# A two-layer hybrid encoder trunk on one core: tiles moved by 128 bytes, the high halves' products first, key tiles evicted in pairs

## The chip, the cores and the metric

One Trainium2 chip, one of its cores. The metric is the device time of one execution in microseconds, the median of several runs. Lower is better.

## What is computed

Two layers, each a chain of five stages on x (512 tokens, 1024 channels): a half-step SwiGLU, a mixer of three branches, a cross-attention into 256 memory tokens, a second half-step SwiGLU, and a layer norm behind each of the four residual sums.

```python
for l in range(DEPTH):                                   # DEPTH = 2
    x = layer_norm(ALPHA * x + 0.5 * swiglu(x, ffn_w12[l, 0], ffn_w3[l, 0]), ...)   # norm 0
    y = hybrid_mixer(x, ...)          # gated delta rule, RG-LRU, chunked attention, gates, w_branch, w_out
    x = layer_norm(ALPHA * x + y, ...)                                              # norm 1
    x = layer_norm(ALPHA * x + memory_cross_attention(x, mem, ...), ...)            # norm 2
    x = layer_norm(ALPHA * x + 0.5 * swiglu(x, ffn_w12[l, 1], ffn_w3[l, 1]), ...)   # norm 3
```

Everything is float32 in the reference. The kernel multiplies in a reduced float32 (fp32r): each operand is split into a high part and the rest, and a product of two is high times high, plus low times high, plus high times low, three matmuls into the same PSUM bank.

## The kernel before

**Operands.** The activations x lie as eight k tiles ("rows" below) of 128 channels by 512 tokens: `xf` whole, `xh` the high part, `xl` the rest. The weights come as a stream of 496 units of 128 x 1024 in the order of use. SP loads a unit into one of four slots of `raw`, GpSimd (`split`, L526) writes its high part to `wh` (L527) and the rest to `wl` (L529), and TensorE uses it. GpSimd may split a unit once the unit three places ahead of it has begun on TensorE (`unit_begun`, L538): then the slot's old unit is done.

**Products.** `three` (L546) issues, for one row and one output tile, `wh` with `xh`, `wh` with `xl`, `wl` with `xh`, the first name being the stationary tile and the second the moving one (the profile prints the moving tile first: `xh,wh`). `unit` (L556) does that for the rows of a unit, and a whole output tile of 128 x 512 is 24 products over eight rows. Four output tiles lie in the four banks of `acc`.

**Behind a layer norm** (`first_four`, L583) the rows of x come one by one: VectorE scales and centres a row (L1556, L1559), ScalarE applies gain and bias and writes `xh` (L1170, L1173), VectorE writes `xl` (L1552). TensorE then goes row by row over four output tiles at once, three products each. It waits for the row's `xl` before the first of them. Only in the last row does it reach the first product of tiles 1 to 3 that counts as "begun". `first_four` is called nine times: for the first feed-forward's up projection (`ffn_up0`, once at the start of the program and once behind norm 3), for `att_qk` behind norm 0, for the first four query tiles (`x_qa`) behind norm 1, for `ffn_up1` behind norm 2. A small product (`ba_product`) follows `att_qk`; in the feed-forwards the fifth tile follows at once.

**Norm 1** has company: TensorE computes the eight key tiles of the memory (`mem_k`, 256 columns, one unit each) beside it, and ScalarE evicts key tile n behind row n (`key_out`, L1408). `x_qa` begins once all eight are evicted, since it takes all four banks. It is followed by the scores and by the memory's values (`mem_v`, eight units, each used by 12 products, moving `wh`/`wl` against stationary `meh`/`mel`).

**Other users of the helpers.** The down projections (`ffn_down`, 22 rows of `hh`/`hl`), `mix_out` (`mh`/`ml`) and `x_out` (`oh`/`ol`) wait per row for the low part, before the row's first product. The mixer's branch projections read `yah`/`yal` and `ych`/`ycl`.

**Places in memory.** Tiles are laid into a partition's bytes in the order of the code, each starting at a multiple of 32. In the built program before, `xh` starts at byte 32896, `xl` at 49280, `wh` at 82048, `wl` at 98432, `const` at 114816; all of these leave 128 when divided by 256. `tmp0` starts at 120544 (leaves 224), and the other `tmp`, `y_sum` and `sq_sum` likewise. `hh` starts at 134144, `hl` at 179200, `ych` at 134144, `ycl` at 150528, `yah` at 173568, `yal` at 181760, `mh` at 189952, `ml` at 206336, `meh` at 142336, `mel` at 150528, `oh` at 183296, `ol` at 199680; all of these leave 0. Every row or column block inside a tile is a multiple of 256 bytes further on, so it leaves the same.

## Time and profile before

| | |
|---|---|
| median of 3 runs | 3358.19 us (3356.82 to 3361.05) |
| the profiled execution | 3360.91 us, its span 3359.1 us |
| TensorE busy | 94% of the span, 14648 matmuls |
| GpSimd, VectorE, ScalarE busy | 52%, 47%, 22% |
| mean granted TensorE clock | 0.974 of full |

A profile's row of a group gives its busy time, the mean of one instruction and the idle time before it. A matmul's modelled end lies behind the start of the next one, so the time per product is read from the distance of starts, or from a piece of the chain of waits divided by its count. The chain of waits is the work that ended last, followed back; in a window of it each piece has its start, its length and what it was.

### The profile page before, as it was taken

Reading aid. Unit: us, or ns where it says so; the run is one execution under the profiler, and the core shown is the slowest. Engines: PE = TensorE matmul, PEld = TensorE weight load, DVE = VectorE, ACT = ScalarE, POOL = GpSimd, SP = SyncE. Lnnn points to the kernel's source line nnn. Section 1 sums busy time; section 2 is a strip of 40 time slices with the busy share of each in tenths; the row PEclk is TensorE's granted clock in tenths of the full one; section 3 lists DMA queues with packets and bytes.
Section 4 is the critical chain, followed back from the end, with each engine's and each line's share of the span. In section 5 each row is a group of like instructions: output and inputs, shape, how many; then the busy total and the mean of one; then the engine's idle time right before and its main releaser. Section 6 shows DMA issues by size and latency. Waiting matters only on the chain.

```text
span 3359.1 us, 42233 instructions
## 1 busy us (share of the span) xinstructions
PE 3171.9 (94%) x14648; PEld 2553.5 (76%) x14648; DVE 1563.8 (47%) x1950; ACT 722.2 (22%) x1293; POOL 1763.4 (52%) x1003
## 2 busy tenths in 40 slices
PE   6999999889999898999999999998999998989996
PEld 5888765678887767888778887656888887778885
DVE  3332446855546435332244323658555373443323
ACT  1110113322221222110021102243222212221101
POOL 5666552433346655666656664424333567456662
PEclk9999999999999999999999999998999999999998
DMA  3223221111122222232222232211111223222231
GB/s 134 94 99 100 85 88 38 63 56 49 54 77 93 90 80 76 100 100 95 99 83 94 100 101 85 69 51 63 51 52 56 88 86 110 68 75 100 94 100 50
DMA packets 78864, 272.62 MB, mean 81 GB/s; under 512 B 8176, under 2 KB 12560, under 8 KB 78736
## 3 DMA queue, kind: packets, MB, share of 16 engines
q1 hardware_dynamic: 73504, 264.27, 23.7%
q10 hardware_dynamic: 5088, 5.96, 0.6%
q8 instruction: 84, 1.38, 0.2%
q0 software_dynamic: 144, 0.66, 0.0%
q14 instruction: 44, 0.36, 0.0%
HBM read 268.73 MB, written 2.12 MB: 81 GB/s over the span
## 4 chain that ended last, share of the span: by engine, by line
PE 82%; DVE 8%; issue 6%; POOL 2%; ACT 1%; DMA 0%; DVEq 0%; POOLq 0%; ACTq 0%; SPq 0%
PE acc L544 72%; PE aux L544 9%; POOL wl L529 1%; DVE dc L1634 1%; POOL wh L527 1%; DVE xl L1501 1%; DVE tmp L1689 1%; DVE dc L1632 1%; PE aux L707 1%; DVE xf L1556 0%; DMA raw<-in_stream 0%; ACT tmp L1135 0%; DVE lc L1695 0%; DVE li L1694 0%; DVE tmp L1872 0%
## 5 line engine op out<-in xcount | busy, mean ns | idle before, releaser
L527 POOL TENSOR_SCALAR wh<-raw 128x1024 fp32r<-128x1024 f32 x496 | 541.7, 1092 | 1505.1 <-PE acc L544 757.2
L529 POOL TENSOR_TENSOR wl<-raw,wh 128x1024 fp32r<-128x1024 f32 x496 | 1222.5, 2465 | 41.4
L544 PE MATMUL acc<-xh,wh 128*128 128x512 f32 x2432 | 993.2, 408 | 81.8 <-POOL wl L529 37.4
L544 PE MATMUL acc<-xh,wl 128*128 128x512 f32 x2432 | 960.4, 395 | 0.0
L544 PE MATMUL acc<-xl,wh 128*128 128x512 f32 x2432 | 960.3, 395 | 0.0
L544 PEld LDWEIGHTS acc<-xh,wh 128*128 128x128 f32 x2432 | 464.6, 191 | 211.0 <-issue 65.1
L544 PEld LDWEIGHTS acc<-xh,wl 128*128 128x128 f32 x2432 | 464.2, 191 | 100.8
L544 PEld LDWEIGHTS acc<-xl,wh 128*128 128x128 f32 x2432 | 465.4, 191 | 91.2 <-issue 2.9
L544 PE MATMUL acc<-hh,wl 128*128 128x512 f32 x704 | 278.1, 395 | 0.0
L544 PE MATMUL acc<-hh,wh 128*128 128x512 f32 x704 | 278.1, 395 | 0.0
L544 PE MATMUL acc<-hl,wh 128*128 128x512 f32 x704 | 278.1, 395 | 0.0
L1501 DVE TENSOR_TENSOR hl<-tmp,hh 128x512 f32 x88 | 228.3, 2594 | 82.2 <-ACT hh L1135 82.2
L1524 DVE SCALAR_TENSOR_TENSOR xf<-acc,xf 128x512 f32<-128x512 f32 x64 | 44.3, 692 | 383.0 <-PE acc L544 382.8
L1512 DVE TENSOR_TENSOR tmp<-tmp,acc 128x512 f32<-128x512 f32 x88 | 60.5, 688 | 275.8 <-PE acc L544 274.3
L1509 DVE SCALAR_TENSOR_TENSOR tmp<-tmp,acc 128x512 f32<-128x512 f32 x88 | 60.5, 688 | 251.1 <-ACT tmp L1135 251.1
L544 PEld LDWEIGHTS aux<-tmp 128*128 128x128 f32 x1088 | 138.3, 196 | 28.2 <-DVE tmp L1872 21.5
L1135 ACT ACT_TABLE_LOAD x85 | 109.1, 1283 | 223.0 <-PE acc L544 221.5
L544 PEld LDWEIGHTS acc<-hl,wh 128*128 128x128 f32 x704 | 132.1, 188 | 32.2
L544 PEld LDWEIGHTS acc<-hh,wl 128*128 128x128 f32 x704 | 132.1, 188 | 32.1
L544 PEld LDWEIGHTS acc<-hh,wh 128*128 128x128 f32 x704 | 132.1, 188 | 32.0
L544 PE MATMUL aux<-tmp 128*128 128x128 f32 x1088 | 142.1, 281 | 14.0 <-DVE tmp L1872 13.6
L1135 ACT ACTIVATE tmp<-xf 128x512 f32<-128x512 f32 x56 | 35.4, 633 | 539.0 <-DVE xf L1524 539.0
(266 smaller groups left out, 3780.3 us busy)
## 6 DMA issues: line engine op xcount, KB each, us to landing
raw<-in_stream SPq DMA_DIRECT2D x496, 512.0 KB, 3.4
xf<-in_xT SPq DMA_DIRECT2D x1, 2048.0 KB, 10.1
bias<-rel_scratch ACTq DMA_DIRECT2D x2, 1024.0 KB, 5.4
mraw<-in_memT ACTq DMA_DIRECT2D x2, 1024.0 KB, 5.2
out_xT<-xf SPq DMA_DIRECT2D x1, 2048.0 KB, 7.1
gate_w<-in_gate_w ACTq DMA_DIRECT2D x2, 512.0 KB, 3.5
const<-in_const POOLq DMA_DIRECT2D x1, 640.0 KB, 8.1
sc<-in_ba_w ACTq DMA_DIRECT2D x2, 256.0 KB, 2.6
```

Source lines behind the costliest of these rows:

```text
L527: pool.tensor_scalar(wh[:, s, :], raw[:, s, :], 1.0, 0.0, ALU.mult, ALU.add).then_inc(hi_step, 1)
L529: pool.tensor_tensor(wl[:, s, :], raw[:, s, :], wh[:, s, :].bitcast(F32), ALU.subtract).then_inc(unit_split, 1)
L544: return pe.matmul(out, w, x, start=start, stop=stop, skip_group_check=True)
L707: last = pe.transpose(aux[:, 2 + n % 2, j * P:(j + 1) * P], sc[:, i, j * P:(j + 1) * P], ident)
L1135: return act.activation(out, in_, func, **kw)
L1501: return tt_(dst, whole, high.bitcast(F32), ALU.subtract)
L1509: stt_(tmp[1][:, :], tmp[0][:, :], 1.0, acc[:, 2 * m, :], ALU.add, ALU.mult).then_inc(freed_d.sem, 1)
L1512: tt_(tmp[2][:, :], tmp[1][:, :], acc[:, 2 * m + 1, :], ALU.mult).then_inc(freed_d.sem, 1)
L1524: stt_(xf[:, d, :], acc[:, d % 4, :], factor, xf[:, d, :], ALU.mult, ALU.add).then_inc(freed_d.sem, 1)
L1632: return ts_(dst, src, weight(3), None, ALU.mult)
L1634: return stt_(dst[:, n:], src[:, 0:SEQ - n], weight(3 - n), dst[:, n:], ALU.mult, ALU.add)
L1689: link(dve.reciprocal(tmp[0][:, :], tmp[0][:, :]))
```

## The change

Four edits.

- A filler of 160 bytes stands behind `par`, and the filler of 32 bytes before the feed-forward's tiles is gone. `tmp`, `y_sum`, `sq_sum` and the small tiles behind them move by 160 bytes (`tmp0` to 120704, leaving 128), and everything from `hh`/`ych` on by 128 bytes (`hh` to 134272, leaving 128, and so with all the others named above). `xf` to `par` stay.
- `three` issues `wh` with `xh`, `wl` with `xh`, `wh` with `xl`. Where a row may not be there yet, TensorE waits for its high part before the first product and for its low part before the third.
- `first_four` goes over rows 0 to 5 with two products per tile (8 a row), and does the four low products of row k behind the eight of row k + 1. Rows 6 and 7 are then done tile by tile, six products each, and a tile's six begin with the product that counts as begun for tiles 1 to 3.
- Behind norm 1's row 3 ScalarE evicts key tiles 3 and 4, behind row 4 tiles 5 and 6, behind row 5 tile 7, and none behind rows 6 and 7.

```diff
+KEYS_OUT = {0: (0,), 1: (1,), 2: (2,), 3: (3, 4), 4: (5, 6), 5: (7,)}
...
         par = sb("par", [P, PAR])
+        sb("par_fill", [P, 40])
...
-        sb("line_fill", [P, 8])
...
-            def three(out, w_hi, w_lo, x_hi_, x_lo_, start, stop, begins=False):
+            def three(out, w_hi, w_lo, x_hi_, x_lo_, start, stop, begins=False, low_ready=None):
                 first = mm(out, w_hi, x_hi_, start, False)
                 if begins:
                     first.then_inc(unit_begun, 1)
-                mm(out, w_hi, x_lo_, False, False)
-                return mm(out, w_lo, x_hi_, False, stop)
+                mm(out, w_lo, x_hi_, False, False)
+                if low_ready is not None:
+                    low_ready()
+                return mm(out, w_hi, x_lo_, False, stop)
...
-            def x_ready(l, norm):
-                return lambda k: pe.wait_ge(x_lo.sem, x_lo.at(l, (norm - 1) * KD + k + 1))
+            def halves_ready(l, hi, lo, at):
+
+                def ready(k):
+                    pe.wait_ge(hi.sem, hi.at(l, at + k + 1))
+                    return lambda: pe.wait_ge(lo.sem, lo.at(l, at + k + 1))
+                return ready
...
-                ready = x_ready(l, norm)
-                for k in range(KD):
-                    ready(k)
+                ready = halves_ready(l, x_hi, x_lo, (norm - 1) * KD)
+                together = KD - 2
+                def low_row(k):
+                    low_ready[k]()
+                    for n in range(4):
+                        mm(acc[:, n, :], wh[:, n, k * P:(k + 1) * P], xl[:, k, :], False, False)
+
+                low_ready = {}
+                for k in range(together):
+                    low_ready[k] = ready(k)
+                    c = slice(k * P, (k + 1) * P)
                     for n in range(4):
                         if k == 0:
                             unit_here(l, UNIT0[name] + n)
-                        c = slice(k * P, (k + 1) * P)
-                        last = three(acc[:, n, :], wh[:, n, c], wl[:, n, c], *of_x(k), k == 0, k == KD - 1,
-                                     begins=k == (KD - 1 if n else 0))
-                        if k == KD - 1:
-                            last.then_inc(acc_ready.sem, 1)
+                        first = mm(acc[:, n, :], wh[:, n, c], xh[:, k, :], k == 0, False)
+                        if k == 0 and n == 0:
+                            first.then_inc(unit_begun, 1)
+                        mm(acc[:, n, :], wl[:, n, c], xh[:, k, :], False, False)
+                    if k:
+                        low_row(k - 1)
+                low_row(together - 1)
+                for n in range(4):
+                    unit(acc[:, n, :], n, range(together, KD), together, of_x, False, True,
+                         ready if n == 0 else None, begins=n > 0).then_inc(acc_ready.sem, 1)
...
-            def key_out(l, n):
-                tile_ready(l, "mem_k", n)
-                fn(xk[:, n, :], acc[:, n % 4, 0:MEM], ACT.Copy).then_inc(freed_a.sem, 1)
+            def keys_out(l, row):
+                for n in KEYS_OUT.get(row, ()):
+                    tile_ready(l, "mem_k", n)
+                    fn(xk[:, n, :], acc[:, n % 4, 0:MEM], ACT.Copy).then_inc(freed_a.sem, 1)
```

The same pair of waits (`halves_ready`) replaces the one wait in `ffn_down` (`hh`/`hl`), `mix_out` (`mh`/`ml`) and `x_out` (`oh`/`ol`).

**On TensorE, from the last key tile to `x_qa`.** A product reads moving tile, stationary tile; what it waits for stands in brackets. Before:

```order
L544 MATMUL acc<-mel,wh 128x256
L544 MATMUL acc<-meh,wl 128x256
L575 REGISTER_ALU
L554 REGISTER_ALU [waits x_lo,freed_a]
L544 MATMUL acc<-xh,wh 128x512 [waits unit_split]
L544 MATMUL acc<-xl,wh 128x512
L544 MATMUL acc<-xh,wl 128x512
L554 REGISTER_ALU
L544 MATMUL acc<-xh,wh 128x512 [waits unit_split]
```

And now:

```order
L545 MATMUL acc<-mel,wh 128x256
L581 REGISTER_ALU
L557 REGISTER_ALU [waits x_hi,freed_a]
L545 MATMUL acc<-xh,wh 128x512 [waits unit_split]
L545 MATMUL acc<-xh,wl 128x512
L557 REGISTER_ALU
L545 MATMUL acc<-xh,wh 128x512 [waits unit_split]
L545 MATMUL acc<-xh,wl 128x512
```

Each of the four units is awaited in row 0, and between two such waits stand two products where three stood. The low product of row 0 has gone behind row 1.

**On TensorE, the end of row 1 in the changed `first_four`**, four low products of row 0 in one row of the listing, and row 2 behind them:

```order
L545 MATMUL acc<-xh,wh 128x512
L545 MATMUL acc<-xh,wl 128x512
L545 MATMUL acc<-xl,wh 128x512 [waits x_lo]
L545 MATMUL acc<-xl,wh 128x512 x3
L545 MATMUL acc<-xh,wh 128x512 [waits x_hi]
```

**On ScalarE, norm 1 from the key eviction behind row 3 on.** Before, one key tile (`xk`) behind each row:

```order
L1135 ACTIVATE xk<-acc 128x256 [waits acc_ready]
L1135 ACTIVATE xf<-xf,par 128x512 [waits centred]
L1135 ACTIVATE xh<-xf 128x512 [waits affine]
L1139 REGISTER_ALU
L1135 ACTIVATE xk<-acc 128x256 [waits acc_ready]
L1135 ACTIVATE xf<-xf,par 128x512 [waits centred]
L1135 ACTIVATE xh<-xf 128x512 [waits affine]
```

And now:

```order
L1153 ACTIVATE xk<-acc 128x256 [waits acc_ready]
L1157 REGISTER_ALU
L1153 ACTIVATE xk<-acc 128x256 [waits acc_ready]
L1153 ACTIVATE xf<-xf,par 128x512 [waits centred]
L1153 ACTIVATE xh<-xf 128x512 [waits affine]
L1157 REGISTER_ALU
L1153 ACTIVATE xk<-acc 128x256 [waits acc_ready]
L1157 REGISTER_ALU
L1153 ACTIVATE xk<-acc 128x256 [waits acc_ready]
```

The last eviction stands behind row 5 now, with rows 6 and 7 behind it.

## Rows read from the trace of the kernel before

**Rows 1.** The page's chain that ended last: share of the span by engine.

```profile
PE 82%; DVE 8%; issue 6%; POOL 2%; ACT 1%; DMA 0%; DVEq 0%; POOLq 0%; ACTq 0%; SPq 0%
```

**Rows 2.** Chain in windows of ffn_up, ffn_down, mix_out, x_out: start us, us, what.

```profile
1719.82 20.40 PE acc L544 x90
...
359.92 20.30 PE acc L544 x87
...
1069.89 20.23 PE acc L544 x87
...
1275.00 12.08 PE acc L544 x52
```

**Rows 3.** Groups by line, one of `hh`'s three: busy us, mean ns | idle us before.

```profile
L544 PE MATMUL acc<-hh,wh 128*128 128x512 f32 x704 | 278.1, 395 | 0.0
```

**Rows 4.** Chain in a window of att_v (moving `wh`, stationary `xh`).

```profile
462.42 21.58 PE acc L544 x95
```

**Rows 5.** TensorE's timeline in mem_v: start us, us, engine line op.

```profile
1188.20 0.39 PE L544 MATMUL acc<-wl,meh 128*128 128x512 f32 x1
...
1190.52 0.39 PE L544 MATMUL acc<-wh,mel 128*128 128x512 f32 x1
```

**Rows 6.** Groups by line: VectorE reading and writing `tmp`.

```profile
L1512 DVE TENSOR_TENSOR tmp<-tmp,acc 128x512 f32<-128x512 f32 x88 | 60.5, 688 | 275.8 <-PE acc L544 274.3
```

**Rows 7.** TensorE's timeline, end of `ffn_up1`'s first four tiles and the fifth's start.

```profile
1324.29 0.39 PE L544 MATMUL acc<-xh,wh 128*128 128x512 f32 x1
1324.52 0.39 PE L544 MATMUL acc<-xl,wh 128*128 128x512 f32 x1
...
1326.10 0.39 PE L544 MATMUL acc<-xh,wl 128*128 128x512 f32 x1
1328.44 0.57 PE L544 MATMUL acc<-xh,wh 128*128 128x512 f32 x1 [1.95 <-POOL wl L529]
```

**Rows 8.** GpSimd's timeline there.

```profile
1324.88 1.07 POOL L527 TENSOR_SCALAR wh<-raw 128x1024 fp32r<-128x1024 f32 x1 [18.47 <-PE acc L544]
```

**Rows 9.** Busy us (count) of PE, PEld, DVE, ACT, POOL, then granted clock, DMA share, GB/s.

```profile
1301.50:1304.80 3.30, 3.19 (x8) 2.53 (x9) 3.23 (x4) 1.96 (x3) 2.13 (x2) 0.50 0.00 0
...
1325.40:1328.70 3.30, 1.35 (x6) 0.83 (x5) 1.38 (x2) 1.54 (x3) 3.22 (x3) 1.00 0.00 0
1328.80:1332.10 3.30, 3.30 (x9) 2.61 (x8) 2.23 (x3) 1.08 (x3) 3.22 (x2) 0.50 0.48 159
1332.20:1335.50 3.30, 3.30 (x16) 2.74 (x15) 1.40 (x1) 0.00 (x0) 3.22 (x2) 1.00 0.45 159
```

**Rows 10.** Timeline behind norm 0: VectorE's first `xl`, TensorE's first and tenth product.

```profile
406.49 0.69 DVE L1501 TENSOR_TENSOR xl<-xf,xh 128x512 fp32r<-128x512 f32 x1 [0.22 <-ACT xh L1135]
...
407.31 0.79 PE L544 MATMUL acc<-xh,wh 128*128 128x512 f32 x1 [3.09 <-DVE xl L1501]
...
412.16 0.50 PE L544 MATMUL acc<-xh,wh 128*128 128x512 f32 x1 [1.03 <-POOL wl L529]
```

**Rows 11.** Norm 1: ScalarE, TensorE's first `x_qa` product, GpSimd's last two `wl`.

```profile
1128.41 0.37 ACT L1135 ACTIVATE xk<-acc 128x256 f32<-128x256 f32 x1
1130.96 0.81 ACT L1135 ACTIVATE xf<-xf,par 128x512 f32<-128x512 f32 x1 [2.18 <-DVE xf L1559]
...
1136.22 0.37 ACT L1135 ACTIVATE xk<-acc 128x256 f32<-128x256 f32 x1
...
1136.72 0.79 PE L544 MATMUL acc<-xh,wh 128*128 128x512 f32 x1 [7.38 <-ACT xk L1135]
...
1134.48 2.35 POOL L529 TENSOR_TENSOR wl<-raw,wh 128x1024 fp32r<-128x1024 f32 x1
1138.97 2.37 POOL L529 TENSOR_TENSOR wl<-raw,wh 128x1024 fp32r<-128x1024 f32 x1
```

**Rows 12.** TensorE's timeline: a `mem_v` unit awaited; `mix_out`'s row 4 awaited.

```profile
1166.85 0.50 PE L544 MATMUL acc<-wh,meh 128*128 128x512 f32 x1 [0.45 <-POOL wl L529]
...
1055.91 0.50 PE L544 MATMUL acc<-mh,wh 128*128 128x512 f32 x1 [2.04 <-DVE ml L1501]
```

More of the change, by code:

```diff
@@ L558, in unit @@
                 for n, k in enumerate(k_tiles):
-                    if ready is not None:
-                        ready(k)
+                    low_ready = None if ready is None else ready(k)
                     c = slice((at + n) * P, (at + n + 1) * P)
                     last = three(out, wh[:, s, c], wl[:, s, c], *rhs(k), start and n == 0,
-                                 stop and n == len(k_tiles) - 1, begins=begins and n == 0)
+                                 stop and n == len(k_tiles) - 1, begins=begins and n == 0, low_ready=low_ready)
                 return last
@@ L586, in first_four @@
                 free_bank(l, name, 0)
-                ready = x_ready(l, norm)
-                for k in range(KD):
-                    ready(k)
+                ready = halves_ready(l, x_hi, x_lo, (norm - 1) * KD)
[8 more added lines that the diff above has]
+                    c = slice(k * P, (k + 1) * P)
                     for n in range(4):
@@ L640, in ffn @@
                         simple_tile(l, up, n, i=i)
-                def inner_ready(k):
-                    pe.wait_ge(inner_lo.sem, inner_lo.at(l, which * KF + k + 1))
+                inner_ready = halves_ready(l, inner_hi, inner_lo, which * KF)
                 def tile(i, n):
@@ L1034, in o_ready @@
             def o_ready(l):
-                return lambda k: pe.wait_ge(xo_lo.sem, xo_lo.at(l, k + 1))
+                return halves_ready(l, xo_hi, xo_lo, 0)
             def out_ahead(l, n, head):
@@ L1119, in _ @@
                     l, "mix_out", lambda k: (mh[:, k, :], ml[:, k, :]),
-                    lambda k: pe.wait_ge(merged_lo.sem, merged_lo.at(l, k + 1))), lambda l: memory_keys(l, slice(0, 1)))
+                    halves_ready(l, merged_hi, merged_lo, 0)), lambda l: memory_keys(l, slice(0, 1)))
                 memory_keys(l)
@@ L1481, in _ @@
                 out_projection(l, "mix_out", 1)
-                layer_norm(l, 1, key_out)
+                layer_norm(l, 1, keys_out)
                 cross_attention(l)
```

## The prediction

> **What bounds the kernel now.** I read the chain of waits by engine first: TensorE holds 82% of it, VectorE 8, "issue" 6 [rows 1]. A microsecond taken from TensorE's products, or from its idle time between stages, comes off the end; what GpSimd, VectorE or ScalarE save counts only where TensorE stands idle for them. So two questions remain: what one product costs, and where TensorE stands.
>
> The cost of a product is read from stretches in which the chain is nothing but products. For the up projection it is 20.40 us / 90 = 0.2267 us. For the down projection, the same size and clock, it is 20.30 / 87 = 0.2333; for `mix_out` 20.23 / 87 = 0.2325, for `x_out` 12.08 / 52 = 0.2323 [rows 2]. The modelled length hides this: 395 ns for a down projection's product [rows 3]. What separates 0.2267 from 0.2333? At 0.2267 both operands lie at places that leave 128 when divided by 256; at 0.2323 to 0.2333 one operand leaves 128 and one leaves 0. Which is moving and which stationary seems not to matter: with `wh` moving against `xh` (both 128) 21.58 / 95 = 0.2272 [rows 4]; with `wh` or `wl` moving against `meh` or `mel` (which leave 0) ten starts span 1190.52 - 1188.20, 0.232 each [rows 5].
>
> **Part 1, the tiles moved.** After the change every operand of a three-part product leaves 128. I take 0.2267 us for all of them.
> - `hh`/`hl`: three groups of 704 [rows 3], 2112 products x 0.0066 us [rows 2] = 13.9 us. All on the path; the chain there holds nothing else.
> - `mh`/`ml`: 8 tiles x 24 x 2 layers = 384 x 0.0058 = 2.2 us. `oh`/`ol`: 384 x 0.0056 = 2.2 us.
> - the mixer's branches: 24 tiles of 12 products x 2 layers = 576, priced like `hh`. Those of the first branch (192) close the mixer and lie on the path, 1.3 us; the other 384 fill TensorE between VectorE's steps, and I count half, 1.3 us.
> - keys and values of the memory: nothing here, since TensorE waits for other engines there (part 3).
> - `tmp` now begins at another place too. VectorE takes 688 ns reading it at its old place [rows 6] and 0.69 us for `xl` from `xf` and `xh`, which leave 128 [rows 10]: no gain, no loss.
>
> Sum: -20.9 us. Bounds: -22.2 with all of the fillers; 0 if the place is not the cause. That a new place could be worse than the old I exclude only by rows: no pair that leaves 128 twice takes longer.
> The Trainium skill speaks against this term ("SBUF — State Buffer", "Who interferes with whom"): TensorE has two independent read ports, one for the moving operand and one for the weights, and never waits on anyone. By it a shift by 128 bytes buys 0 and the sum would be rival A's. It has no word on where in a line of memory an operand begins, and it doesn't explain rows 2.
>
> **Part 2, order within three products.** Each has its own weight load. The step between two products with the same weights takes 0.23 us (1324.29 to 1324.52), and the mean of the eight steps to 1326.10, most of them to other weights, 0.226 [rows 7]. So weights that alternate more often cost nothing.
>
> **Part 3, `first_four`.**
> *The fifth tile.* In the feed-forwards its unit may be split only once tile 1 has begun. That product starts 9 before the end, at 1324.29; GpSimd starts at 1324.88 [rows 8], and TensorE gets the unit at 1328.44, 4.15 us behind 1324.29, while its products end at about 1326.10 + 0.23 = 1326.33: 2.11 us idle [rows 7]. Now tile 1 begins 18 products before the end, 9 x 0.2267 = 2.04 us earlier. The unit comes 0.07 us behind the end. Gain 2.04 us. The idle time also costs clock: behind it comes a stretch at 0.50 of full speed (1.2 GHz) with 9 products, then one at 1.00 (2.4 GHz) with 16 [rows 9]; seven fewer by 0.2267 is 1.6, and I take 1.5 as the wait is in the neighbouring stretch. Four calls have it (both `ffn_up0`, both `ffn_up1`; the trace has three more such waits): 4 x 3.54 = -14.2 us. Behind `att_qk` a small product covers the wait: 0.
> *The start behind a norm.* TensorE waits for `xl` of row 0 (406.49 + 0.69), starts at 407.31, issues nine products at the low clock and stands for the fourth unit until 412.16 [rows 10]. That unit's split hangs on TensorE's first product, 4.85 us earlier. Now the first product needs `xh` alone: 0.82 us earlier, and so the fourth unit. But six products are done before it instead of nine, so three more lie behind: + 3 x 0.2267 = 0.68. Net -0.14. Then the clock: nine products in a row brought it back to 1.00 by the time the unit came (0.50 with 8 of them, [rows 9]). Six, and a wait of 2.3 us instead of 1.0, may not. Cost between 0 and a stretch and a half, 2.7 us; I take 1.2, less than one, because products then follow without a break. Net +1.1 each, five such starts (norms 0, 2, 3; not the last): +5.5 us.
> *The program's start*: units arrive one by one, three more products lie behind the fourth: +0.7 us.
>
> **Part 4, norm 1.** TensorE starts `x_qa` at 1136.72 behind an idle time of 7.38 us, so it finished the keys at 1129.3; what it waited for is ScalarE's last eviction (1136.22), behind row 7. The new place is behind row 5, whose eviction is at 1128.41 [rows 11]: the key tile is ready at 1129.3, evicted by 1129.7, and TensorE may begin at 1129.9, 6.8 us earlier. This does not carry through. Row 0 of `first_four` walks over four units, and GpSimd delivers the third at 1134.48 + 2.35 = 1136.8. The fourth, now not held by the gate, follows at once, by 1140.4 instead of 1141.3 [rows 11]. So -0.9, +0.68 for three products, +1.1 for the clock: +0.9 at the end of `x_qa`. The scraps of work between 1130 and 1140 are two products per 3.9 us. Behind it, `mem_v` waits again and again for GpSimd (0.45 us [rows 12], four such waits, 1.6 in all, over 0.1 each), whose first split there hangs on the begin of tile 1: 2.04 earlier against the end. 0.9 - 2.04 = -1.1, and TensorE's waits leave room for about that: -1.0 per layer, -2.0 us. Bounds per layer: +1.5 (clock late, waits unchanged) and -2.4.
> *The extra evictions* cost ScalarE 0.37 us each behind rows 3 and 4 [rows 11]; it idles 2.18 us before the next row, and the chain there runs over VectorE and GpSimd: 0.
>
> **Part 5, the other waits.** `mix_out` stands 2.04 us for a row's low part [rows 12]; two products go before the wait now: -0.45, twice, -0.9. In `ffn_down` and `x_out` the low parts are there in time: 0. The additional waits are one semaphore test per row beside 0.68 us of products: 0.
>
> **Sum.** -20.9 - 14.2 + 5.5 + 0.7 - 2.0 - 0.9 = -31.8 us. The profiled execution took 3360.9, so 3329.1; the median of the runs is 2.7 lower, so **3326.4 us**. Its own range: best -22.2 - 14.2 - 0.7 - 4.8 - 0.9 + 0.7 = -42, worst with all clock terms at their ends -20.9 - 8.2 + 13.5 + 0.7 + 3.0 = -12; the ends won't fall together, I hold 3317 to 3337.
>
> **Rivals.** About 0.2% (6.7 us) is what a measurement of this kernel can tell from no change.
> - **A: the place buys nothing.** For it: all tiles that come with the longer products also start at byte 134144 or above, all those with the shorter ones below 115000, so height separates them as well as the remainder does, and the rule of the page says the same. Against it: no mechanism in the rows would make height matter. Only parts 3 to 5 are left, -10.9: 3347.3.
> - **B: the place pays, the clock eats the rest.** Starts cost 2.7 each (+8.0), norm 1 gives +1.5 per layer (+5.0), and half of the low stretches behind the fifth tile return elsewhere (+3.0): -15.8, 3342.4.
> - **C: the edit at the fifth tile doesn't do what it says.** The split could be held by something else, a unit not loaded in time. Against it: in the stretch of that split no transfer is under way (DMA share 0.00 [rows 9]), so what it needs is there. Then -17.6: 3340.6.
> - **D: slower.** At each start behind a norm and at `x_qa` the clock stays at the low level after the fourth unit. A product costs about 0.40 us then (3.19 us for 8 [rows 9]) instead of 0.227, so 90 of them cost 15.6 us more. It decides from 31.8 / 7 = 4.5 us per start over what I assumed, some 26 products. With all 90: 7 x 15.6 = +109, less the 8.2 assumed, 3326.4 + 101 = 3427. For it: a norm leaves TensorE idle and the first burst is shorter. Against it: after nine products the clock was back [rows 9].
>
> **Chances.** Forecast 0.64, A 0.17, B 0.11, C 0.06, D 0.02. Range 3312 to 3346: it holds the forecast, B and C; A lies just above it. Faster by over 0.2% are forecast, A, B and C but for a tail where A meets late clocks: 0.92. Same 0.06, slower 0.02.
>
> **What would show it.** Chain stretches of `ffn_down` at 0.2267 per product (right) or 0.2333 (A). No 1.9 us wait of TensorE for `wl` ahead of the fifth tile, and no 0.50 stretch behind it (C if it is there). First product behind a norm right after `xh`, six products, a wait of some 2.3 us; the clock stretch tells B and D. `x_qa`'s first product near 1130 of the old count, its fourth unit 0.9 us earlier only. I am wrong in the main if the median is above 3346 or the down projections keep their pace.

## The result, and the profile after

The changed kernel takes 3332.26 us (median of 4 runs, 3330.97 to 3333.01) where the kernel before, run beside it, takes 3359.22: 27.0 us less, a ratio of 0.9917 with a 95% interval of 0.9906 to 0.9929. The forecast was 3326.4 in a range of 3312 to 3346. The profiled execution took 3332.1 us with a span of 3330.3, against 3360.9 and 3359.1 before.

The share of the chain is TensorE's as before [rows 1], a point more of it:

```profile
PE 83%; DVE 8%; issue 5%; POOL 2%; ACT 1%; DMA 0%; DVEq 0%; POOLq 0%; SPq 0%; ACTq 0%
```

**The cost of a product.** The chain of the changed kernel in windows of `ffn_up`, `ffn_down` and `x_out` (start, length, what):

```profile
59.97 20.17 PE acc L545 x89
...
339.90 20.17 PE acc L545 x89
...
1261.81 14.28 PE acc L545 x63
```

20.17 / 89 and 14.28 / 63 are 0.2267 us each: down projection and `x_out` now run at the pace of the up projection [rows 2]. The modelled length of a product fell from 395 to 389 ns [rows 3]:

```profile
L545 PE MATMUL acc<-hh,wh 128*128 128x512 f32 x704 | 273.9, 389 | 0.0
```

In `mix_out` TensorE's timeline gives (1082.07 - 1060.99) / 93 = 0.2267 as well, 93 steps from product to product lying between these two starts:

```profile
1060.99 0.39 PE L545 MATMUL acc<-mh,wh 128*128 128x512 f32 x1
...
1082.07 0.39 PE L545 MATMUL acc<-mh,wh 128*128 128x512 f32 x1
```

**The fifth tile** [rows 7 to 9]. Timeline and stretches of the changed kernel at the end of `ffn_up1`'s first four tiles in layer 0; the columns of the stretches are those of [rows 9]:

```profile
1315.56 1.05 POOL L528 TENSOR_SCALAR wh<-raw 128x1024 fp32r<-128x1024 f32 x1 [18.55 <-PE acc L545]
...
1318.83 0.39 PE L545 MATMUL acc<-xl,wh 128*128 128x512 f32 x1
1319.15 0.50 PE L545 MATMUL acc<-xh,wh 128*128 128x512 f32 x1
```

```profile
1316.40:1319.70 3.30, 3.30 (x15) 2.49 (x14) 1.40 (x3) 1.54 (x4) 3.22 (x3) 1.00 0.00 0
1319.80:1323.10 3.30, 3.30 (x16) 2.73 (x15) 2.19 (x4) 0.84 (x2) 3.22 (x3) 1.00 0.46 159
```

The step across the border is 0.32 us instead of 0.2267, so 0.1 us of waiting is left of 2.1, and the stretch behind holds 16 products at 1.00 where there were 9 at 0.50.

**The start behind a norm** [rows 9, 10]. TensorE's timeline behind norm 0, and two stretches behind norm 2:

```profile
400.90 0.49 PE L545 MATMUL acc<-xh,wh 128*128 128x512 f32 x1 [2.37 <-ACT xh L1153]
405.12 0.50 PE L545 MATMUL acc<-xh,wh 128*128 128x512 f32 x1 [2.57 <-POOL wl L530]
```

```profile
1293.50:1296.80 3.30, 1.00 (x3) 0.28 (x1) 3.25 (x5) 2.13 (x4) 3.22 (x2) 0.50 0.00 0
1297.10:1300.10 3.00, 3.00 (x7) 2.44 (x8) 2.94 (x5) 1.68 (x3) 0.00 (x0) 0.50 0.53 173
```

The first product hangs on `xh`, the wait for the fourth unit is 2.57 us instead of 1.03, and behind it seven products run at 0.50 (1.2 GHz).

**Norm 1** [rows 11] **and `mix_out`** [rows 12]. TensorE's timeline in `x_qa`, GpSimd's next split, and the wait in `mix_out`:

```profile
1121.64 0.49 PE L545 MATMUL acc<-xh,wh 128*128 128x512 f32 x1 [0.55 <-ACT xk L1153]
1124.56 0.50 PE L545 MATMUL acc<-xh,wh 128*128 128x512 f32 x1 [2.19 <-POOL wl L530]
1128.44 0.79 PE L545 MATMUL acc<-xh,wh 128*128 128x512 f32 x1 [3.15 <-POOL wl L530]
1132.63 0.80 PE L545 MATMUL acc<-xh,wh 128*128 128x512 f32 x1 [2.96 <-POOL wl L530]
```

```profile
1151.42 1.05 POOL L528 TENSOR_SCALAR wh<-raw 128x1024 fp32r<-128x1024 f32 x1 [18.85 <-PE acc L545]
```

```profile
1050.38 0.50 PE L545 MATMUL acc<-ml,wh 128*128 128x512 f32 x1 [1.68 <-DVE ml L1520]
```

Counted from norm 1's first product, `x_qa` begins 8.1 us earlier (30.73 us behind it for 38.87) and crawls: two products per unit, the third unit 3.9 us and the fourth 4.2 us behind the one before. Behind the fourth, GpSimd has nothing to do for 18.85 us.

**Where the 28.8 us of the spans went.** A stage is the distance between the first products of two stages in TensorE's timeline. Attention runs from the first score to the first gate product of the mixer, the mixer from there to `mix_out`.

| stages | change in us | forecast |
|---|---|---|
| 4 down projections, 123.19 to 119.68 each | -14.0 | -13.9 |
| `mix_out` and `x_out`, both layers | -2.8, -1.9 | -3.1, -2.2 |
| mixer, both layers | -1.9 | -2.6 |
| program start, and norms 0, 2, 3 with what follows up to `ba_product` or the down projection | -7.7 | -8.0 |
| norm 1 to the end of `mem_v`, both layers | -2.8 | -2.0 |
| attention, layer 0 and layer 1 | 0.0, +3.0 | 0 |
| last norm; small rest | -0.9; +0.2 | 0 |

### The profile page after: what moved, and what is told of

It is laid out like the page before. It is cut to its first block, busy times and chain, and to the rows that moved or that the text cites. A ratio compares the mean times of both kernels' runs of the same rounds, so it can differ in the third digit from the quotient of the medians.

```text
span 3330.3 us, 42233 instructions
## 1 busy us (share of the span) xinstructions
PE 3146.7 (94%) x14648; PEld 2546.5 (76%) x14648; DVE 1570.7 (47%) x1950; ACT 723.0 (22%) x1293; POOL 1764.2 (53%) x1003
## 4 chain that ended last, share of the span: by engine, by line
PE 83%; DVE 8%; issue 5%; POOL 2%; ACT 1%; DMA 0%; DVEq 0%; POOLq 0%; SPq 0%; ACTq 0%
PE acc L545 73%; PE aux L545 9%; DVE dc L1653 1%; POOL wl L530 1%; DVE sq_sum L1555 1%; POOL wh L528 1%; DVE dc L1651 1%; PE aux L725 1%; DVE xf L1540 0%; DVE xf L1543 0%; DVE y_sum L1549 0%; DMA raw<-in_stream 0%; ACT tmp L1153 0%; DVE lc L1714 0%; DVE li L1713 0%
## 5 line engine op out<-in xcount | busy, mean ns | idle before, releaser
L545 PE MATMUL acc<-xl,wh 128*128 128x512 f32 x2432 | 929.5, 392 | 0.0
L1520 DVE TENSOR_TENSOR hl<-tmp,hh 128x512 f32 x88 | 235.0, 2670 | 82.0 <-ACT hh L1153 82.0
L545 PEld LDWEIGHTS aux<-tmp 128*128 128x128 f32 x1088 | 138.2, 195 | 28.3 <-DVE tmp L1891 21.8
L545 PE MATMUL aux<-tmp 128*128 128x128 f32 x1088 | 142.1, 281 | 14.2 <-DVE tmp L1891 13.8
```

The costliest lines, as they stand in the source:

```text
L545: return pe.matmul(out, w, x, start=start, stop=stop, skip_group_check=True)
L1520: return tt_(dst, whole, high.bitcast(F32), ALU.subtract)
```

## The experiments

Ten kernels ran, each four to nine times, with the kernel before beside it (`e3_places` once). The first three ask what a place costs.

**`e1_tiles_only`: the fillers alone**, on the kernel before.

```diff
         par = sb("par", [P, PAR])
+        sb("par_fill", [P, 40])
...
-        sb("line_fill", [P, 8])
```

> The kernel before with the two fillers alone; order of products, waits and evictions stay as before. Forecast's theory (a pair of operands that both leave 128 costs 0.2267 us a product, a pair of 0 and 128 costs 0.2333): 20.9 us less than before (bounds 13.9, only hh and hl, to 22.2), ffn_down's products 0.2267 us apart. Rival A (the place buys nothing): 0 +- 2 us, ffn_down's products still 0.2333 apart.

Measured: 3342.67 us against 3359.79, 17.1 less; ratio 0.9947 (0.9933 to 0.9961). The chain in `ffn_down` gives 51.23 / 226 = 0.2267:

```profile
339.78 51.23 PE acc L544 x226
```

Rival A has fallen. But it is 3.8 us short of 20.9. The stages name it: down projections -14.0 as forecast, `x_out` -1.8 for 2.2, mixer -1.5 for 2.6, and `mix_out` 0.6 us *longer* per layer instead of 1.1 shorter. There TensorE waits for row 4's low part, 2.04 us before and 2.11 now, and in this run a stretch of 3.41 us at 0.50 lies behind that wait. `e3_places` (below) shows what such a stretch costs: up to its bursts it is the kernel before, instruction for instruction, and the stretch behind the wait is there in layer 0 and absent in layer 1:

```profile
1054.00:1057.30 3.30, 3.30 (x9) 2.60 (x8) 3.27 (x3) 0.00 (x0) 0.00 (x0) 0.50 0.34 134
2711.00:2714.30 3.30, 3.30 (x16) 2.69 (x15) 3.27 (x3) 0.00 (x0) 1.10 (x1) 1.00 0.32 118
```

`mix_out` takes 48.65 us there in layer 0 and 46.94 in layer 1, 1.7 us apart with nothing changed. So the 0.6 us of `e1_tiles_only` are 1.1 gained by the place and 1.7 lost to the clock. Why the stretch comes in one layer and not in the other, the runs don't show.

**`e7_all_leave_0`: every operand leaves 0**, on the kernel before.

```diff
+        sb("x_fill", [P, 32])
         xf = sb("xf", [P, KD, SEQ])
...
-        sb("line_fill", [P, 8])
+        sb("line_fill", [P, 8 + 32])
```

> The kernel before with a filler of 128 bytes ahead of xf and 128 bytes more ahead of hh: xf to par now leave 0, and so do hh, mh, oh, yah, meh as they did before, all 256 bytes further on; order, waits and evictions stay as before. If equal remainders are what counts: as in e1, 17 us less than before, ffn_down's products at 0.2267. If both must leave 128: no gain, 0 +- 2 us, and the up projections too slow to 0.2333 (3 x 11 tiles of 24 products and more, +25 us).

Measured: 3342.39 us (3337.21 to 3344.29) against 3360.26, 17.9 less, ratio 0.9947 (0.9933 to 0.9960); products of `hh` and of `xh` at a median distance of 0.227 us. What counts is not 128 but that both operands leave the same.

**`e3_places`: bursts at chosen places**, appended to the kernel before.

```diff
+            moving = hh[:, :, :].rearrange("p k t -> p (k t)")
+            still = hl[:, :, :].rearrange("p k t -> p (k t)")
+            for a, b in PLACES:
+                mm(aux[:, 1, 0:64], still[:, 0:P], moving[:, 0:64])
+                for n in range(30):
+                    mm(aux[:, 0, :], still[:, b // 4 + P * (n % 8):b // 4 + P * (n % 8) + P],
+                       moving[:, a // 4 + SEQ * (n % 4):a // 4 + SEQ * (n % 4) + SEQ])
```

Four more bursts have 256 columns, 40 in all.

> The kernel before with 36 bursts of 30 products behind its last product (some 250 us more, their result unused), a burst for each pair of places (remainder by 256 of the moving and of the stationary operand), all from tiles above byte 134144, into one bank. Theory 1 (equal remainders): every pair with equal remainders 0.2267 us apart, (0,0) and (64,64) too; all others 0.2333. Theory 2 (both must leave 128): only (128,128) 0.2267, (0,0) at 0.2333 or more. Theory 3 (a remainder of 0 in either costs): (32,32), (64,64), (128,64) 0.2267. Rival A (height in memory): no burst below 0.2323, since all read above 134144.

Measured, a burst's fifth and thirtieth product in TensorE's timeline, for the pairs (0, 0), (32, 0), (64, 0), (128, 128) of moving and stationary remainder:

```profile
3335.24 0.39 PE L546 MATMUL aux<-hh,hl 128*128 128x512 f32 x1
3340.93 0.39 PE L546 MATMUL aux<-hh,hl 128*128 128x512 f32 x1
...
3342.20 0.40 PE L546 MATMUL aux<-hh,hl 128*128 128x512 f32 x1
3348.04 0.39 PE L546 MATMUL aux<-hh,hl 128*128 128x512 f32 x1
...
3349.31 0.39 PE L546 MATMUL aux<-hh,hl 128*128 128x512 f32 x1
3355.04 0.39 PE L546 MATMUL aux<-hh,hl 128*128 128x512 f32 x1
...
3420.28 0.39 PE L546 MATMUL aux<-hh,hl 128*128 128x512 f32 x1
3425.96 0.40 PE L546 MATMUL aux<-hh,hl 128*128 128x512 f32 x1
```

Divided by 25 steps: 227.6, 233.6, 229.2 and 227.2 ns, to within 0.4 ns, since starts are shown to 0.01 us. All bursts of 512 columns, from unrounded starts:

| moving minus stationary, by 256 | pairs tried | ns per product |
|---|---|---|
| 0 | (0,0) twice, (32,32), (64,64), (128,128) twice, (256,0), (0,256) | 226.7 to 227.7 |
| 64 | (64,0), (192,128), (0,192), (128,64) | 228.8 to 229.0 |
| any other multiple of 32 | the other 24 | 232.5 to 234.4 |

All of it lies above byte 134144, so height plays no part, and theory 2 falls with (0,0) and (32,32), theory 3 with (0,0) at 227 and (128,32) at 233.7. Theory 1 holds but for a middle step that nobody expected: 64 more for the moving operand costs 2 ns, 64 less costs 6. With 256 columns all four pairs take 119 to 120 ns, so a product of half the width pays nothing, matching or not.

The Trainium skill ("SBUF — State Buffer", "Who interferes with whom") lets TensorE's two reads be independent and TensorE wait on nobody; by that rule the table would have one row. The measurement decides: where the two operands lie against each other costs up to 6 ns of 233. By what mechanism, the runs don't show.

The next three take the order apart.

**`e2_order_only`: the change without its fillers.**

```diff
         par = sb("par", [P, PAR])
-        sb("par_fill", [P, 40])
...
+        sb("line_fill", [P, 8])
```

> The change without its fillers: every tile lies where it lay before, order, waits and evictions are the change's. Forecast's theory: 10.9 us less than before by the sum of parts 3 to 5, or 27.0 - 20.9 = 6.1 by what the change as a whole gave; ffn_down's products 0.2333 us apart. Rival A, or a theory in which order and waits made the whole gain: 27 us less than before. If the two edits help each other (a shorter product lets a wait end later), e1 and e2 together give less than 27.

Measured: 3350.68 us against 3359.79, 9.1 less, ratio 0.9973 (0.9963 to 0.9982). That lies between the 10.9 and the 6.1 of the expectation. Its profiled span is 7.8 us shorter, and 10.7 without attention, which took 2.9 us more. 17.1 + 9.1 = 26.2 of the change's 27.0: in the total the two halves nearly add up. Stage by stage they don't. `mix_out`: +0.6 us per layer by the fillers, -0.5 by the order, -1.4 by both, for the change lacks the low stretch of `e1_tiles_only`. Norm 1 to the end of `mem_v`: 0 by the fillers, +0.1 per layer by the order, -1.4 by both; the low stretch in the key tiles lasts 6.83 us in `e2_order_only` and 3.41 in the change. So the sum of the halves is partly luck.

**`e5_last_rows_only`: rows 6 and 7 tile by tile**, on the kernel before.

```diff
-                for k in range(KD):
+                together = KD - 2
+                for k in range(together):
...
-                        last = three(acc[:, n, :], wh[:, n, c], wl[:, n, c], *of_x(k), k == 0, k == KD - 1,
-                                     begins=k == (KD - 1 if n else 0))
-                        if k == KD - 1:
-                            last.then_inc(acc_ready.sem, 1)
+                        three(acc[:, n, :], wh[:, n, c], wl[:, n, c], *of_x(k), k == 0, False, begins=k == 0 and n == 0)
+                for n in range(4):
+                    unit(acc[:, n, :], n, range(together, KD), together, of_x, False, True,
+                         ready if n == 0 else None, begins=n > 0).then_inc(acc_ready.sem, 1)
```

> The kernel before with one edit: in first_four rows 6 and 7 are done tile by tile, so that tile 1 begins 18 products before the end instead of 9; order within three products, waits, starts, evictions and places stay. Forecast's term for the fifth tile: 4 x 3.54 = 14.2 us less, since nothing of the starts is touched. Rival 1 (only the wait of 2.04 goes, the clock it cost comes back elsewhere): 4 x 2.04 = 8.2 less. Rival 2 (the 7.7 us that the change as a whole gained at these places is all there is, and the starts cost nothing): 7.7 less. The stage from a norm's sums to the down projection tells each of the four apart: -3.5, -2.0 or -1.6 us behind norm 2.

Measured: 3343.68 us (3338.3 to 3348.8) against 3360.26, 16.6 less, ratio 0.9950 (0.9937 to 0.9964). The stages split it. At the four fifth tiles: -3.5 (program start), -1.7 and -1.8 (behind norm 2), -4.1 (behind norm 3), in sum -11.1. `mem_v` -2.0 per layer, because its first unit comes 2.04 us earlier against `x_qa`'s end. And -3.2 in layer 0's attention, which this edit doesn't touch (see `e8_attention_later`). Behind layer 1's norm 0, where no fifth tile follows, it lost 1.0. Its starts are those of the kernel before, nine products ahead of the fourth unit, and yet in three of its five starts behind a norm the clock came back only 8.5 to 8.7 us behind the first product, where in the kernel before it took 3.2 to 3.4 us each time. Behind layer 0's norm 2, this kernel's stretch of 3.8 to 7.1 us behind the first product, and that of the kernel before (3.3 to 6.6 us), which follows the first stretch of [rows 9]:

```profile
1296.90:1300.20 3.30, 2.66 (x7) 1.82 (x6) 3.27 (x5) 1.81 (x3) 1.03 (x1) 0.50 0.31 88
```

```profile
1304.90:1308.20 3.30, 2.26 (x11) 1.53 (x10) 3.27 (x5) 1.45 (x2) 1.50 (x1) 1.00 0.18 53
```


**`e4_row0_three`: nine products ahead of the fourth unit**, on the change.

```diff
                         mm(acc[:, n, :], wl[:, n, c], xh[:, k, :], False, False)
-                    if k:
+                        if k == 0:
+                            if n == 0:
+                                low_ready[0]()
+                            mm(acc[:, n, :], wh[:, n, c], xl[:, k, :], False, False)
+                    if k > 1:
                         low_row(k - 1)
```

> The change, but in row 0 each tile's low product stands directly behind its two high ones, as before the change; so nine products instead of six precede the wait for the fourth unit. The forecast's theory of the start (three more products behind the fourth unit at 0.68 us, and 1.2 us of clock): 5 x 1.9 + 0.7 = 10 us less than the change, 3322. Rival (the longer burst does not bring the clock back, only the three products count): 6 x 0.68 = 4 us less, 3328. Rival 2 (the low products of row 0 come late, TensorE waits for them): no less than the change, 3332.

Measured: 3324.10 us (3323.6 to 3325.4), 8.2 less than the change. By the total the forecast's theory looks right, and it isn't: attention gave 3.3 and 2.9 of it, `x_qa` 0.7 per layer, and the starts that the edit is about, all six together, 1.3 instead of 10. Behind norm 2 the longer burst did not bring the clock back; two stretches of this kernel, the first nine products and those behind the unit:

```profile
1287.10:1290.40 3.30, 3.26 (x8) 2.59 (x9) 3.23 (x6) 2.52 (x4) 2.21 (x2) 0.50 0.00 0
1293.00:1296.30 3.30, 3.30 (x9) 2.62 (x8) 3.23 (x7) 2.00 (x3) 0.00 (x0) 0.50 0.54 164
```

Nine products, and still 0.50 until 1296.4, which is 9.2 us behind the first one; the change with its six products was back at 1.00 at 1300.2, 7.8 us behind its first. In `e4_row0_three` it takes that long at all five norms, 8.6 to 9.4 us. What the three products saved behind the unit went into the longer low stretch.

**`e6_keys_by_row`: the evictions as before**, on the change.

```diff
-KEYS_OUT = {0: (0,), 1: (1,), 2: (2,), 3: (3, 4), 4: (5, 6), 5: (7,)}
+KEYS_OUT = {k: (k,) for k in range(8)}
```

> The change, but one key tile is evicted behind each row of norm 1 as before the change, so x_qa begins some 7 us later than in the change (behind row 7). Forecast's theory (x_qa's end hangs on GpSimd's last unit, not on its first product): the fourth unit is split 0.9 us later, but the low clock of the scattered products (10.2 us in the change, 4.3 before) shrinks: between -1.1 and +0.9 us per layer against the change, 3330 to 3334 in all. Rival (the earlier begin is worth what it looks like, 7 us per layer): 3346.

Measured: 3332.47 us against the change's 3332.26. Counted from norm 1's first product, `x_qa` begins 6.6 us later and the scores 0.1:

```profile
1128.59 0.79 PE L545 MATMUL acc<-xh,wh 128*128 128x512 f32 x1 [7.18 <-ACT xk L1153]
1133.23 0.80 PE L545 MATMUL acc<-xh,wh 128*128 128x512 f32 x1 [1.72 <-POOL wl L530]
```

The fourth unit comes at 1133.23 for 1132.63; norm 1 itself began 0.3 us later in this run, so 0.3 us are left. The pairs of evictions are worth nothing as long as `x_qa` takes a row across all four units.

**`e8_attention_later`: attention, 2.72 us later**, on the change.

```diff
                     unit_here(l, UNIT0["att_v"] + n)
+                    if n == 0:
+                        for e in range(12):
+                            extra = mm(acc[:, 0, :], xh[:, 0, 0:P], wh[:, 0, 0:BRW], True, False)
+                            if e == 0:
+                                extra.then_inc(unit_begun, 1)
...
-                            if t == 0 and m == 0:
+                            if t == 0 and m == 0 and n:
```

> The change with 12 extra products (2.72 us of TensorE) per layer ahead of the attention's values; their result is overwritten. In 20 attention stages of ten profiles the low clock behind the scores' start lasted 3.41 us where it began 1.30 us or more behind the first score, and 10.24 us where it began 0.61 to 1.25 behind it; the stage took 114.7 or 117.8 us with nothing else changed. In the change it began at 1.25 and 0.71. Theory (the phase against the steps of the clock sets it): 2.72 us later the next step falls some 1.9 us behind the first score in both layers, both stages take 114.7, and of 5.4 us of extra work 6.2 come back: 3332 - 0.8 = 3331.5. Rival (something else in the stage sets it): 5.4 us more, 3337.7, both stages still at 117.8.

Measured in the profile: both stages 114.7 us, the low stretch beginning 1.58 and 1.35 us behind the first score; span 3330.6, 0.3 more than the change for 5.4 us of added work. The stretches of the change behind the first scores, layer 0 and 1, then those of this kernel, layer 0:

```profile
487.90:498.00 10.10, 10.10 (x21) 5.41 (x20) 5.10 (x15) 2.43 (x9) 3.40 (x2) 0.50 0.16 54
2129.70:2139.80 10.10, 10.04 (x20) 5.31 (x19) 5.63 (x16) 1.97 (x7) 3.40 (x2) 0.50 0.17 54
```

```profile
491.90:495.20 3.30, 3.30 (x9) 2.04 (x7) 2.56 (x9) 0.82 (x4) 1.70 (x2) 0.50 0.00 0
495.30:502.10 6.80, 6.80 (x29) 4.41 (x28) 3.90 (x11) 2.83 (x9) 1.60 (x1) 1.00 0.23 77
```

The median of the five runs is 3335.96 (3331.3 to 3338.1), 3.7 above the change; the profiled one took 3332.4. The median lies nearer to the rival's 3337.7 than to 3331.5. That spread, and a profiled execution at its lower end, suggest that the phase (where the work falls against the clock's steps) differs from run to run and that the profile shows one case of it. So one profile bears the mechanism out in both layers; a gain in the median is not shown. The kernel before has the two kinds side by side, low for 10.24 us in layer 0 and for 3.41 in layer 1:

```profile
492.50:502.60 10.10, 10.10 (x20) 5.47 (x21) 5.28 (x15) 2.13 (x8) 3.40 (x2) 0.50 0.17 54
2151.40:2154.70 3.30, 3.30 (x7) 1.82 (x6) 3.05 (x9) 1.08 (x4) 1.20 (x2) 0.50 0.02 5
2154.80:2161.50 6.70, 6.70 (x28) 4.19 (x27) 3.54 (x10) 2.83 (x9) 2.12 (x1) 1.00 0.24 78
```

The rows agree with what the Trainium skill says ("TensorE: Matmul & The Clock Gate", Part 1): the watch over TensorE's activity runs freely, is not reset by a kernel, and so the point at which the clock changes depends on where the work falls in it.

**`v1_stairs`: another order in `first_four`**, on the change. Behind a norm the first rows go over the three tiles whose units are there; `x_qa` goes tile by tile.

```diff
+def first_order():
+    rows = []
+    for k in range(3):
+        rows += [("h", k, n) for n in range(3)]
+        if k:
+            rows += [("l", k - 1, n) for n in range(3)]
+    rows += [("l", 2, n) for n in range(3)]
+    rows += [("h", k, 3) for k in range(3)] + [("l", k, 3) for k in range(3)]
+    for k in range(3, KD - 2):
+        rows += [("h", k, n) for n in range(4)]
+        if k > 3:
+            rows += [("l", k - 1, n) for n in range(4)]
+    return rows + [("l", KD - 3, n) for n in range(4)]
+FIRST_FOUR = [first_order(), []]
+TAIL = [KD - 2, 0]
...
+                for part, k, n in FIRST_FOUR[name == "x_qa"]:
+                    (high if part == "h" else low)(k, n)
```

("h": a tile's two high products of a row, "l": its low one, "TAIL": the row from which tiles are done one by one.)

> The change with another order in first_four. Behind norms 0, 2 and 3: rows 0 to 2 for the first three tiles, which need nothing of the fourth unit, then these rows for tile 3, then on as in the change. In x_qa: tile 0 with all its rows, then tile 1, and so on, since its units come one by one every 3.9 us and GpSimd stands still for 18.9 us behind the fourth. Expected: the wait for the fourth unit behind a norm (2.57 us) goes and the low stretch behind it gets shorter: -3 us at each of five starts; x_qa ends some 9 us earlier in each layer; the program's start -2 us. In all 3332 - 15 - 18 - 2 = 3297. Rival (the memory's values then wait for GpSimd, whose split takes 3.45 us per unit against 2.8 of products): half of x_qa's gain comes back, 3306. Rival (at the starts the clock stays low as long as in e4, 9 us, and eats what the wait gave): 3310.

Measured: 3294.31 us (3291.0 to 3295.0), 38.0 less than the change; against before a ratio of 0.9803 (0.9789 to 0.9816). Program start and norm starts give 19.3 us by their stages, norm 1 to the end of `mem_v` 8.3 and 8.4, attention 2.1. Neither rival came: `mem_v` itself got shorter, 25.1 for 26.8 us. Two stretches behind norm 2:

```profile
1274.90:1278.10 3.20, 3.15 (x7) 2.51 (x8) 3.17 (x5) 2.42 (x4) 2.08 (x2) 0.50 0.00 0
1278.20:1281.50 3.30, 3.30 (x16) 2.70 (x15) 3.27 (x4) 1.53 (x3) 1.58 (x1) 1.00 0.12 37
```

No wait, and 1.00 comes back 3.2 us behind the first product instead of 7.8. At the five norms it is 2.8 to 3.9 us in four and 6.2 in one.

**`v2_two_tiles`: two more changes of order**, on `v1_stairs`.

```diff
-FIRST_FOUR = [first_order(), []]
-TAIL = [KD - 2, 0]
+FIRST_FOUR = [first_order(), [(part, k, n) for n in range(2) for k in range(KD - 2) for part in "hl"]]
+TAIL = [(KD - 2,) * 4, (KD - 2, KD - 2, 0, 0)]
+LOW_LATER = 3
...
+                        mm(acc[:, n, :], wl[:, n, c], rhs(k)[0], False, False)
+                        if k >= LOW_LATER:
+                            late[k - LOW_LATER]()
+                            d = k - LOW_LATER
+                            mm(acc[:, n, :], wh[:, n, d * P:(d + 1) * P], rhs(d)[1], False, False)
```

> v1_stairs with two more changes of order. x_qa takes rows 0 to 5 of tiles 0 and 1 before rows 6 and 7 of tile 0, since v1 waits 2.56 us for row 6's low part; mix_out's first tile issues each row's low product three rows later, since it waits 1.67 us for row 4's. Expected: -2.5 and -1.5 us per layer, 3294 - 8 = 3286. Rival (x_qa then runs into its third unit, which comes at the same time as before): -1.5 per layer from mix_out alone, 3291. Each may move by 3.1 us with the clock of the attention.

Measured: 3281.70 us (3276.9 to 3282.6), 12.6 less than `v1_stairs`, 50.6 less than the change; against before a ratio of 0.9767 (0.9754 to 0.9781). It beats both kernels. The profiled executions lie 17.5 us apart. From `x_qa`'s first product to the scores it takes 21.89 us, where 96 products by 0.2267 are 21.8, so this stage is at its floor: 4.8 less per layer, twice the expectation. `mix_out` gave 0.2 instead of 1.5. The longest wait shrank from 1.67 to 0.34 us, but the tile still needs all eight low parts, and VectorE delivers the last ones no faster. Its last four low products in `mix_out`'s first tile start 0.6 us apart instead of 0.2267; VectorE's last four low parts in one row, and TensorE's products behind the wait, three in one row:

```profile
1035.59 4.70 DVE L1560 TENSOR_TENSOR ml<-xf,mh 128x512 fp32r<-128x512 f32 x4
...
1038.54 1.70 PE L563 MATMUL acc<-ml,wh 128*128 128x512 f32 x3 [0.34 <-DVE ml L1560]
```

Over the whole stage TensorE is 1.78 us above 192 products at 0.2267, where in `v1_stairs` it is 1.99. The rest came unasked: 4.0 us in the attention of both layers, which has the short stretch twice, and 4.5 in the mixer, with 6.8 us less at 0.50 per layer. Whether that too is phase wasn't tried.

## Why the prediction was right, and where it was wrong

- **The likeliest case came**, rivals A to D did not: `ffn_down` at 0.2267 (against A), norm starts 0.2 us and not 2.7 dearer and norm 1 a gain (against B), no wait and no low stretch ahead of the fifth tile (against C), no start with the clock low through four tiles (against D). The median is 5.9 us above the number.
- **Part 1, -20.9, and part 5, -0.9.** The stages give -20.6 for the -21.8 of both. The pace was right to the last digit; what was wrong is its reason ("both leave 128"): the same remainder counts, 0 and 0 does as well. Part 5 measured -0.9 in `e2_order_only`, just as forecast. The missing 1.2 us are in the mixer (-1.9 for -2.6) and in `mix_out` and `x_out` (-4.7 for -5.3).
- **Part 2, 0.** Nothing speaks against it: `ffn_up`'s pace is 0.2267 in both orders. It was not tried alone.
- **Part 3, -14.2 and +6.2.** Both terms are too large, and the errors cancel: -8.0 forecast, -7.7 measured. That the sum fits so well is luck. Alone, the fifth tile gave 11.1 (`e5`), so the step "I take 1.5" for the clock held at the program's start and behind norm 3 but not behind norm 2, where 1.7 us came of 3.5. The change against `e5` leaves +2.5 for the starts, of which +1.7 is the program's own. The five norm starts, "Net +1.1 each", measure +0.7, -0.7, +0.1, +0.2 and +0.5, +0.2 in the mean; the -0.7 is the 1.0 us that `e5` itself had lost at layer 1's norm 0, and against the kernel before the two starts behind norm 0, which have no fifth tile, measure +0.6 and +0.35. The reason given, that nine products in a row bring the clock back and six may not, is what failed: in `e4` nine did not at any norm, and in `e5` the same nine of the kernel before did at two norms and did not at three.
- **The program's start, +0.7**, measured +1.7. The three more products behind the fourth unit are there; the other 1.0 us is clock, a term that the forecast left out. In the change the products are 0.43 us apart until 33.9 us and then 0.23, in the kernel before until 31.7 us: 2.2 us more at half the pace. TensorE's timeline, the change, then the kernel before:

```profile
32.14 0.63 PE L545 MATMUL acc<-xh,wh 128*128 128x512 f32 x1
32.57 0.63 PE L545 MATMUL acc<-xh,wl 128*128 128x512 f32 x1
...
34.33 0.40 PE L545 MATMUL acc<-xh,wh 128*128 128x512 f32 x1
34.56 0.40 PE L545 MATMUL acc<-xh,wl 128*128 128x512 f32 x1
```

```profile
30.87 0.63 PE L544 MATMUL acc<-xh,wl 128*128 128x512 f32 x1
31.30 0.57 PE L544 MATMUL acc<-xh,wh 128*128 128x512 f32 x1
31.70 0.39 PE L544 MATMUL acc<-xl,wh 128*128 128x512 f32 x1
```

The clock's column doesn't show it. It reads 1.00 for the change's stretch too:

```profile
31.50:34.80 3.30, 3.30 (x10) 2.54 (x10) 0.00 (x0) 0.00 (x0) 0.00 (x0) 1.00 0.01 4
```

The trace's first record of the clock begins at 33.9 us in the change (31.7 before), and ahead of a first record the column stands at 1.00. There the distance of starts tells the clock: 0.43 us is also the step in `e1_tiles_only`'s `mix_out`, where the column reads 0.50.
- **Part 4, -2.0**, measured -2.8: +0.6 at the scores instead of +0.9 per layer, and the 2.04 us in `mem_v` came in full, -2.0 (`e5` shows them alone). The +0.6 is luck in part: in `e2_order_only`, the same order at the old places, it is +2.1, with 6.83 us at the low clock in the key tiles for the change's 3.41. That the early begin does not carry through was right, and `e6` shows it.
- **Missing altogether: the attention.** No term touches that stage, and it took 3.0 us more in layer 1, at the low clock for 10.24 instead of 3.41 us. In all profiles here but `v1_stairs`' layer 0 (6.83 us) the low stretch is the long one where it begins 0.6 to 1.25 us behind the first score and the short one where it begins 1.30 or more behind it. These 3.0 us are as large as the whole gap in the profiled execution (3329.1 forecast, 3332.1 measured); the other terms' errors cancel. The other 2.9 of the median's gap: I took the median 2.7 us below the profiled execution, as it was before, and in the change they lie 0.2 apart.

What stays open: why a difference of 64 one way costs 2 ns and the other way 6; why the same instructions get a low stretch in one execution or layer and not in another; and what sets the clock's phase from run to run.

## What to carry to other kernels

Put the moving and the stationary operand of wide products at the same remainder by 256 bytes: here that was worth 6 ns of 233 on each of 3,456 products, for two fillers. Where an engine waits for the n-th of several buffers, first give it all the work that the n - 1 others allow, and signal a buffer free as early as the order of the products lets you: that alone was worth more than the change. Of the 50.6 us of `v2_two_tiles` (55.1 in the profiled spans) some 46 lie in the stages whose order was edited, against 27.0 of the change; the rest came in attention and the mixer, which these edits don't touch. And split every difference by stages before believing it: a total can agree with a theory while a stage that the edit doesn't touch supplied it, as in `e4`, by way of the clock's phase.

## What the runs showed of the hardware

- A product of 512 columns takes 227 ns with both operands at the same remainder by 256, 229 with the moving one 64 further, 233 otherwise; with 256 columns 119 to 120 whatever the places.
- Attention takes 114.7 or 117.8 us in the same instructions, 3.1 us that come and go with shifts of the work ahead of it, as 3.41 or 10.24 us run at the low clock; one stage of 24 lay between (115.8 us, 6.83). `mix_out` has the same: 46.94 or 48.65 us.
- The burst after which TensorE is back at 2.4 GHz is not a number of products: behind a norm six products with 2.57 us of waiting ended up back at 1.00 7.8 us after the first one, nine with 0.64 us of waiting 9.2 us after it, and unbroken work in `v1_stairs` 3.2 us after it. Nor is it the order of products alone: nine products in the same order were back 3.2 us after the first in the kernel before and 8.6 us after it in `e5_last_rows_only`.
- Ahead of its first record the profile shows the clock as 1.00 whatever it is: in the first 33.9 us of the change products of 512 columns start 0.43 us apart, the pace of 0.50.
